# Norm weights and rotary rotation moved from GpSimd to VectorE in a two-layer hybrid decoder trunk

## The reference, cut to what matters

```
def rmsnorm(x, gain):
    xf = x.astype(jnp.float32)
    xf = xf * lax.rsqrt(jnp.mean(xf * xf, axis=-1, keepdims=True) + EPS)
    return xf.astype(x.dtype) * gain

def apply_rope(x, cos, sin):
    x1, x2 = x[..., :half], x[..., half:]
    return jnp.concatenate([x1 * cos - x2 * sin, x1 * sin + x2 * cos], axis=-1)

# A:  o = rmsnorm(o, o_gain) ... ;  return o * silu(g)
# B:  q = rmsnorm(c_q, q_norm_g) @ w_uq ;  kv = rmsnorm(c_kv, kv_norm_g) @ w_ukv
#     q = rmsnorm(q, qk_g[0]) ;  k = rmsnorm(k, qk_g[1])        (8 heads of 64 + 32)
#     the last 32 of q and of k go through apply_rope ;  scores = q . k
# C:  q = rmsnorm(q, qk_g[0]) ;  k = rmsnorm(k, qk_g[1]) ;  scores = q . k ;  o = rmsnorm(o, o_g) * (1 - lam_init)
# D:  q = rmsnorm(q, qk_g[0]) ;  k = rmsnorm(k, qk_g[1]) ;  scores = q . k
```

## Time and profile before

| what | us |
|---|---|
| median of 3 runs | 2605.45 (2600.79 to 2609.75) |
| the profiled execution | 2604.83 |
| its span, first to last instruction | 2603.1 |
| busy: TensorE matmul, VectorE, ScalarE, GpSimd | 2280.1, 1181.0, 807.5, 425.7 |
| steps from `hg_norm` to `dif_post` in layer 0 | 311 to 687 |
| the same steps in layer 1 | 1593 to 1971 |

### The profile page before, as it was taken

How to read it: one execution, slowest core, us unless ns; L and a number is a source line. 1 busy time by engine, 2 the same in 40 slices (tenths; PEclk the granted TensorE clock), 3 DMA queues, 4 the chain that set the end, 5 groups by cost and what they waited for, 6 DMA issues and landing times.

```text
span 2603.1 us, 31879 instructions
## 1 busy us (share of the span) xinstructions
PE 2280.1 (88%) x11806; PEld 1746.5 (67%) x11806; DVE 1181.0 (45%) x2391; ACT 807.5 (31%) x1635; POOL 425.7 (16%) x457
## 2 busy tenths in 40 slices
PE   3999988969899978999759998898798999799996
PEld 2797877856674556767538878677666646467774
DVE  6727665445545531111275476554465364311113
ACT  2423333434442221111224333343444412211111
POOL 1002323020002201123100122320200022011230
PEclk8999988979999988999869998889798999799997
DMA  8232232122228435860263223221231465278402
GB/s 263 73 92 62 92 119 70 45 81 74 73 91 305 180 144 196 304 236 25 73 228 92 79 75 111 90 73 42 69 93 53 161 247 210 97 257 305 144 6 97
DMA packets 202103, 333.65 MB, mean 128 GB/s; under 512 B 31200, under 2 KB 162144, under 8 KB 185696
## 3 DMA queue, kind: packets, MB, share of 16 engines
q1 hardware_dynamic: 179024, 305.32, 34.9%
q0 software_dynamic: 19296, 19.98, 2.4%
q10 hardware_dynamic: 3632, 6.31, 0.6%
HBM read 352.48 MB, written 51.38 MB: 155 GB/s over the span
## 4 chain that ended last, share of the span: by engine, by line
PE 80%; DVE 8%; issue 5%; ACT 3%; DMA 2%; SPq 1%; POOL 1%; POOLq 0%; DVEq 0%; ACTq 0%
PE ps L719 74%; PE ps L717 6%; DVE ring_rounded L1754 1%; DVE ssq L1866 1%; SPq L555 1%; DMA ring<-in_ada_w 1%; DMA M<-h_rows,find_i 1%; DVE nmax L1891 1%; ACT WH_rounded L1335 0%; DVE spare L1736 0%; DMA ring<-in_w_in 0%; DVE ps L1888 0%; DVE X L2272 0%; ACT SC L1414 0%; ACT rsq L1416 0%
## 5 line engine op out<-in xcount | busy, mean ns | idle before, releaser
L719 PE MATMUL ps<-H_rounded,WH_rounded 128*128 128x512 f32 x768 | 309.8, 403 | 0.0
L719 PE MATMUL ps<-WH_rounded,X_rounded 128*128 128x256 f32 (+1 forms) x960 | 281.1, 293 | 28.6 <-issue 28.6
L719 PE MATMUL ps<-X_rounded,WH_rounded 128*128 128x512 f32 x640 | 289.3, 452 | 14.0 <-DVE H_rounded L1859 5.9
L719 PE MATMUL ps<-ring_rounded,X_rounded 128*128 128x256 f32 (+1 forms) x960 | 278.5, 290 | 0.0
L719 PE MATMUL ps<-WH_rounded,H_rounded 128*128 128x256 f32 (+1 forms) x960 | 277.9, 289 | 0.0
L1754 DVE TENSOR_TENSOR ring_rounded<-ring,WH_rounded 128x512 fp32r<-128x512 f32 (+2 forms) x168 | 198.1, 1188 | 169.1 <-ACT WH_rounded L1335 168.6
L719 PE MATMUL ps<-X_rounded,ring_rounded 128*128 128x512 f32 x640 | 254.6, 398 | 0.0
L1335 ACT ACTIVATE WH_rounded<-ring 128x512 fp32r<-128x512 f32 (+2 forms) x168 | 163.6, 983 | 209.3 <-PE ps L719 70.4
L719 PE MATMUL ps<-Y,ring 128*128 128x512 f32 x512 | 221.2, 593 | 1.9 <-ACT Y L1433 1.9
L719 PEld LDWEIGHTS ps<-WH_rounded,X_rounded 128*128 128x128 f32 x960 | 192.3, 200 | 30.4 <-issue 30.2
L719 PEld LDWEIGHTS ps<-ring_rounded,X_rounded 128*128 128x128 f32 x960 | 192.2, 200 | 0.6 <-issue 0.5
(11 more groups left out here) (350 smaller groups left out, 3906.0 us busy)
## 6 DMA issues: line engine op xcount, KB each, us to landing
ring<-in_w_in SPq DMA_DIRECT2D x272, 256.0 KB, 3.9
ring<-in_ada_w SPq DMA_DIRECT2D x128, 256.0 KB, 5.0
ring<-in_w_branch SPq DMA_DIRECT2D x64, 256.0 KB, 5.3
Y<-in_moe_w_gate SPq DMA_DIRECT2D x16, 1024.0 KB, 5.6
ring<-in_moe_w_up SPq DMA_DIRECT2D x16, 1024.0 KB, 5.1
gate_logits<-CM SPq DMA_DIRECT2D x44, 256.0 KB, 2.6
DVt<-gate_logits SPq DMA_DIRECT2D x8, 1024.0 KB, 4.9
SQKV<-gate_logits SPq DMA_DIRECT2D x8, 1024.0 KB, 5.2
```

Of the source, the lines that this page charges most:

```text
L719: ins = nc.tensor.matmul(o, lhsT, rhs, start=start, stop=stop)
```

## The change

GpSimd's part in the list is taken away, and its multiplications are put on VectorE right behind the multiplication by the reciprocal root, each behind a wait on VectorE's own count (`vector_step`). Three further things change:

- The scaled query weights of C, D and of the unrotated 64 features of B are multiplied into the key weights once per layer (3 small instructions ahead of the first `ada`), and the queries get no weights: `dif_norm` weighs 512 columns instead of 1024, `swa_norm` 128 instead of 640, `up` 512 instead of 1536.
- For the rotated 32 features of B the weights are multiplied into the cosine and sine tables once per layer (`rope_tables`, 8 small instructions at the end of `c_norm`), for queries and keys apart. `rope` keeps its six instructions of 256 columns, without the waits between the first four.
- VectorE waits for the sine tables once, behind the first four `ada` steps of layer 0.

```diff
             def head_norm(x, tmp, n, d):
...
-                v.tensor_tensor(x, x, spread(rsq[:, 0:n], d), ALU.mult).then_inc(normed, p.gives(normed))
+                v.tensor_tensor(x, x, spread(rsq[:, 0:n], d), ALU.mult).then_inc(vector_step, p.gives(vector_step))
+                eng.wait_ge(vector_step, p.given(vector_step))
+
+            def weigh_by(x, g, sem):
+                v.tensor_tensor(x, x, g, ALU.mult).then_inc(sem, p.gives(sem))
+
+            def rope_tables():
+                g = heads(row("mla_qk_norm"), 2)
+                lo, hi = g[:, :, NOPE:NOPE + HALF], g[:, :, NOPE + HALF:]
+                for a, (tab, by) in enumerate(((cosT, lo), (sinT, hi), (sinT, lo), (cosT, hi))):
+                    for k in range(2):
+                        v.tensor_tensor(rope_tab[:, :, a, k], tab[:, :, :], repeat(by[:, k], NT), ALU.mult).then_inc(
+                            vector_step, p.gives(vector_step))
+
+            def rope(qk, t):
...
+                for a, x in enumerate((x1, x2, x1, x2)):
+                    tab = rope_tab[:, t, a].unsqueeze(2).to_broadcast([P, 2, HEADS, HALF])
+                    v.tensor_tensor(by_kind(tmp[a]), by_kind(x), tab, ALU.mult).then_inc(
+                        vector_step, p.gives(vector_step))
+                eng.wait_ge(vector_step, p.given(vector_step))
+                v.tensor_tensor(x1, tmp[0], tmp[1], ALU.subtract).then_inc(vector_step, p.gives(vector_step))
+                v.tensor_tensor(x2, tmp[2], tmp[3], ALU.add).then_inc(gained, p.gives(gained))
...
-                elif step_ in ("hg_norm", "dif_post"):
+                elif step_ == "hg_norm":
                     for t in range(NT):
                         head_norm(*norm_of(step_, t))
+                        weigh_by(heads(hgO[:, t], HEADS), repeat(row("hg_onorm"), HEADS), vector_step)
+                        eng.wait_ge(vector_step, p.given(vector_step))
+                        weigh_by(hgO[:, t], TM[:, t, 512:1024], gained)
+                elif step_ == "dif_post":
+                    for t in range(NT):
+                        head_norm(*norm_of(step_, t))
+                        weigh_by(heads(y_tok["diff"][:, t], DH), repeat(row("diff_onorm"), DH), gained)
                 elif step_ == "c_norm":
...
+                    head_norm(*norm_of(step_, 0))
+                    weigh_by(CM[:, :, 0:QR], repeat(row("mla_q_norm"), NT), gained)
+                    head_norm(*norm_of(step_, 1))
+                    weigh_by(CM[:, :, QR:QR + KVR], repeat(row("mla_kv_norm"), NT), gained)
+                    rope_tables()
+                elif step_ == "dif_norm":
                     head_norm(*norm_of(step_, i))
+                    weigh_by(heads(DQK[:, i, 512:1024], 8), repeat(row("diff_qk_norm", 0, HD), 8), gained)
+                elif step_ == "swa_norm":
+                    head_norm(*norm_of(step_, i))
+                    weigh_by(heads(SQKV[:, i, 512:640], 2), repeat(row("swa_qk_norm", 0, HD), 2), gained)
                 elif step_ == "up":
...
                     head_norm(*norm_of("up", i))
+                    weigh_by(qk[:, HEADS:, 0:NOPE], repeat(row("mla_qk_norm", 0, NOPE), HEADS), vector_step)
+                    rope(qk, i)
...
+                for name, n, width in (("mla_qk_norm", QKD, NOPE), ("diff_qk_norm", HD, HD), ("swa_qk_norm", HD, HD)):
+                    v.tensor_tensor(row(name, 0, width), row(name, 0, width), row(name, n, width), ALU.mult).then_inc(
+                        vector_step, p.gives(vector_step))
...
         def _(eng):    # gpsimd
...
-                for st, i in SCHEDULE:
-                    do(st, i)
```

More of the change, by code:

```diff
@@ L2015, in _ @@
                     ada(s, 2, s)
+                if l == 0:
+                    eng.wait_ge(tables_ready, p.next(tables_ready, 2))
                 eng.wait_ge(lamexp_ready, p.next(lamexp_ready))
@@ L2485, in _ @@
             eng.wait_ge(constants_ready, p.given(constants_ready))
[L2487 to L2491, removed]
-                    if after is None and k == len(parts) - 1:
-                        ins.then_inc(gained, p.gives(gained))
-                    else:
-                        ins.then_inc(pool_step, p.gives(pool_step))
-                        eng.wait_ge(pool_step, p.given(pool_step))
-                if after is not None:
-                    after()
@@ L2511, in do @@
-            def do(step_, i):
-                if step_ == "hg_norm":
-                    for t in range(NT):
-                        o = hgO[:, t]
-                        gains([(heads(o, HEADS), repeat(row("hg_onorm"), HEADS))],
-                              lambda: eng.tensor_tensor(o, o, TM[:, t, 512:1024], ALU.mult).then_inc(
-                                  gained, p.gives(gained)))
-                elif step_ == "c_norm":
-                    gains([(CM[:, :, 0:QR], repeat(row("mla_q_norm"), NT))])
-                    gains([(CM[:, :, QR:QR + KVR], repeat(row("mla_kv_norm"), NT))])
-                elif step_ == "up":
-                    qk = heads(qk_tile[i % 2], 2 * HEADS)
-                    p.mark(handed[1])
-                    gains([(qk[:, k * HEADS:(k + 1) * HEADS], repeat(row("mla_qk_norm", k * QKD, QKD), HEADS))
-                           for k in range(2)], lambda: rope(qk, i))
-                elif step_ == "dif_norm":
-                    gains([(heads(DQK[:, i, k * 512:(k + 1) * 512], 8), repeat(row("diff_qk_norm", k * HD, HD), 8))
-                           for k in range(2)])
-                elif step_ == "swa_norm":
-                    gains([(heads(SQKV[:, i, 0:512], 8), repeat(row("swa_qk_norm", 0, HD), 8)),
-                           (heads(SQKV[:, i, 512:640], 2), repeat(row("swa_qk_norm", HD, HD), 2))])
-                elif step_ == "dif_post":
-                    for t in range(NT):
-                        p.mark(handed[t % 2])
-                        gains([(heads(y_tok["diff"][:, t], DH), repeat(row("diff_onorm"), DH))])
@@ L2536, in _ @@
-            eng.wait_ge(tables_ready, p.next(tables_ready, 4))
             p.mark(handed[1])
@@ L2539, in _ @@
                 p.mark(handed[2])
-                eng.wait_ge(rows_ready, p.next(rows_ready))
-                alone()
+                p.mark(handed[1], NT)
+                p.mark(handed[0], 2)
+                p.mark(handed[1], 2)
                 for pr in range(4):
```

26 lines of the change are left out of this document (9 added, 17 removed).

## The result

The changed kernel takes **2614.22 us** (median of 20 runs, 2606.89 to 2627.07); the kernel before, run beside it, 2606.75 (20 runs). The ratio is 1.003, 95% interval 1.0019 to 1.0041: slower by 0.3%, on the side that I forecast, inside the range, and at 7.5 us less than half of the 18.9 that I had summed. The profiled execution takes 2614.76, its span is 2613.0.

The account below looks back on a forecast made before the run. The prediction took VectorE's place in front of TensorE's waits as the bound. Its terms gave 9.2 us per layer, 18.4 for two, plus 0.5 for weight products: 18.9 on 2604.83, forecast 2624 us, range 2611 to 2632.

Parts of the forecast that it names:

- rival B: Idle time ahead of the third projection takes up most of the `hg_norm` delay, clock not lost twice: 2614 us; chance 0.14.
- the prices: An added VectorE multiplication with its wait costs its duration plus 0.03 us: 0.72 for 512 columns, 1.26 for 1024.
- Term 1: `hg_norm`: eight added multiplications less two no longer stretched, fully on the path ahead of the second projection: +3.6 us per layer.
- Term 3: `c_norm`: added weight and table products less stretched instructions, on the path to TensorE's first `up`: +1.0 us per layer.
- Term 5: `dif_norm` and `swa_norm`: -1.35 us at `ada` 3, +0.72 and +0.96 behind it; together +0.3 per layer.
- Term 6: `dif_post`, between differential and window sweeps: 2.9 us added, 0.63 back at a stretched instruction; net +2.25 per layer.
- Term 4: `up` and `turn`: GpSimd's wait becomes a longer wait for ScalarE, VectorE's extra 3.0 us fall in idle time: 0.
- Term 2: Second projection: TensorE runs at a low clock behind its new idle time, +2.0 us per layer, bounds 0 and 3.1.
- Rival A: Not slower: GpSimd was late, `hg_norm` and `c_norm` work fits its time, TensorE gains 7.9 us: 2602.6 us; chance 0.08.

Follow-up runs that it names:

- hg_only: Kernel before with only `hg_norm`'s weights and gate moved to VectorE, the rest on GpSimd with joined weights and weighted tables: 2610.72 us, ratio 1.0007.
- swa_joined: Kernel before with only the window norm's query weights joined into its key weights, all still on GpSimd: 2606.56 us, ratio 1.0001.

## Why the prediction was wrong in its size, and where it was right

The side was forecast and the size was not: 7.5 us instead of 18.9. That 2614 lies inside the range is luck, since the range reaches down to 2611 for the sake of rival B, and my forecast proper began at 2616.

Right were the side, the bound (VectorE's place in front of TensorE's waits), and the prices, as the segments show:

- Term 1, `hg_norm`: 3.6 forecast, 3.66 in every layer of every trace with this step on VectorE. No slack, as read from rows 3 and 5. TensorE idled 2.2 to 3.7 in the four layers, mostly less than the 3.6 that I gave, since its own first projection ended later; the delay of the chain is the 3.66.
- Term 3, `c_norm`: 1.0 forecast, 0.88 measured.
- Term 5: -1.35 at `ada` 3, measured -1.4; the norms behind it +1.7, measured +1.4.
- Term 6, `dif_post`, as far as it prices the idle time: 2.25 forecast, TensorE's idle time grew by 2.25 (6.39 to 8.64).
- Term 4: GpSimd's wait in `turn` did turn into a longer wait for ScalarE. The segment came out 1.65 shorter than the forecast 0, in the mean of four values. Over all seventeen traces it lies between 152.4 and 156.6 with no order that I can name, and the two layers of `dif_joined` alone have 155.8 and 152.6. So this part may be spread, and its cause is open.

Wrong was the clock. Two steps of the sum failed:

1. **Term 2, mis-sized.** "I take 2.0, nearer to the upper one, because the idle time is longer than the one that made that row": measured 0.7 in the mean. In this kernel's first layer the clock stayed at 1.00 behind 2.22 us of idle time; in `hg_only`, behind 2.82 at the same place, the next 11.6 us had 0.85 (the last but two of the numbers, TensorE alone):

```profile
325.20:336.80 11.60, 11.49 (x83) 0.85 0.31 90
```

In the ten layers with this step on VectorE and nothing added, the clock stayed at 1.00 behind 2.22, 2.33 and 2.40 us, and those 11.6 us had 0.76 to 0.85 in the seven layers with 2.57 to 3.69. The segment to `c_norm` took 24.2 in the three and 25.7 to 27.1, mean 26.0, in the seven; with the step on GpSimd it took 24.8. So where the clock fell it cost 1.2, and it fell in three of the four layers of the changed kernel. My row had 0.53 over 6.6 us, a loss of 3.1; 0.85 over 11.6 us is a loss of 1.7. Nor did the loss reach the third projection: TensorE waited for that for 2.88 us in the first layer and 1.12 in the second, and it began 17.1 and 16.8 us behind the second projection.

2. **Term 6 counted the idle time of the hand-over and nothing else.** The window sweep behind it was taken as a fixed length. In the trace that I read it was not: its two layers took 98.0 and 103.2 us with the same instructions, and I looked at the first alone: "The second layer's rows repeat the first's within a few tenths" was not true here. The kernel before had the 103 us form in two of four layers, the changed kernel in none. The length of the low-clock stretch went with the place of the hand-over in all traces but one layer, and moving the hand-over by useless work moved both, so that place is what decides, and the change moved it. What sets the place in a given execution is not shown. That is 1.9 us per layer beyond the 0.6 that I had booked at the stretched instruction.

With these the sum reads, per layer: 9.2 - 1.3 (term 2) - 1.65 (term 4, open) - 1.9 (window sweep) - 0.4 (the rest) = 3.95, for two layers 7.9. The 0.5 for the weight products at a layer's start lies outside these segments, and no run shows it.

Rival B gave 2614, the time that was measured, and that too is chance, for its mechanism did not act: the second projection's delay was not absorbed, and SyncE's loads still hung on its first matmul. Rival A had the wrong place, though not the wrong question: something in this change does make the kernel faster. It is the halved work of the differential norm, and it needs no move to VectorE.

**A version that beats both**: the kernel before with the differential norm's query weights joined into the key weights, still on GpSimd (`dif_joined`, 0.9974; with the window norm's too, `dif_swa_joined`, 0.9963 and 0.9977 in two sets). Some 1.0 us per layer of it is path. The window sweeps, 98.6 and 98.2 against a mean of 101.1 before, hold most of the rest, so a further change ahead of the hand-over can lose it again.

## What to carry to other kernels

Cost a move by what stands between the engine's old and new position and the waits of the bound engine: summed from rows, such prices hold within tenths. When a change is made of a useful and a costly part, time the parts alone: here the algebra alone was worth 4 to 9 us, and the move took more than that back. And before summing, compare the same stage in every layer of the trace of before; where it takes two lengths with the same instructions, a shift of one us can be worth five.

## What was not expected of the hardware

- How long TensorE stayed at 1.2 GHz behind the hand-over, with the same work, went with how long before its first matmul the clock had fallen. In the 34 hand-overs of all seventeen traces: fallen 3.3 us ahead or less, the low clock lasted 3.5 to 4.6 us behind that matmul (13 of 14; once 17, in `swa_joined`); 3.4 to 4.0 us ahead, it lasted 13 to 14 (9 of 9); 4.1 to 4.6 ahead, 9 to 10 (3 of 3); 5.5 or more, 4 to 5 (8 of 8). The idle time was 6.4 us in 22 of them and 8.6 in 12. It did not decide: 13 to 14 us stand behind 6.4 (seven times) and behind 8.6 (twice), and so do the short stretches. The long form cost the window sweep 4 to 5 us.
- At the second projection the clock stayed at 1.00 behind idle times of 2.22 to 2.40 us (3 of 3) and fell behind 2.57 to 3.69 (7 of 7).
- Work that delays VectorE by 1.2 us per layer cost 7.0 us in one kernel and 9.7 in another; taking 2.25 us of idle time away cost 7.
- A wait on VectorE's own count costs 0.12 us, measured by itself.
